# GpSimd subtracts one of the twelve weight splits of each expert

## The reference, cut to what matters

```python
def expert_block(args):
    xblk, e = args
    gu = xblk @ w_gu[e] + b_gu[e]                     # (rows, 1024) @ (1024, 2048)
    x_glu = jnp.minimum(gu[:, :F], SWIGLU_LIMIT)
    x_lin = jnp.clip(gu[:, F:], -SWIGLU_LIMIT, SWIGLU_LIMIT)
    act = x_glu * jax.nn.sigmoid(SWIGLU_ALPHA * x_glu) * (x_lin + 1.0)
    return act @ w_down[e] + b_down[e]                # (rows, 1024) @ (1024, 1024)

y = yb.reshape(P, D) * row_gate[:, None]
out = jax.ops.segment_sum(y, row_tok, num_segments=N + 1)[:N]
```

## Time and profile before

| | us |
|---|---|
| median of 3 runs | 1246.93 (1246.45 to 1248.09) |
| the profiled execution | 1246.31 |
| its span, first to last instruction | 1244.5 |
| VectorE busy | 1148.0 |
| TensorE busy (matmuls) | 1147.7 |
| ScalarE busy | 933.5 |
| GpSimd busy | 517.7 |

### The profile page before, as it was taken

The page is one execution under the profiler, slowest core; times in us unless marked ns, Lnnn a source line. Parts: engine busy times, 40 slices in busy tenths (PEclk is TensorE's granted clock), DMA queues, the critical chain, the costliest instruction groups (busy, mean ns, idle before and its releaser), DMA issues.

```text
span 1244.5 us, 40003 instructions
## 1 busy us (share of the span) xinstructions
PE 1147.7 (92%) x17556; PEld 886.6 (71%) x17557; DVE 1148.0 (92%) x870; ACT 933.5 (75%) x823; POOL 517.7 (42%) x69
## 2 busy tenths in 40 slices
PE   5999999999999999999999999999999999999974
PEld 2445545877777777777777777777777778888741
DVE  5755576999999999999999999999999999999987
ACT  5334444788888888888888888888888888888851
POOL 0110400027777776767766666632300111366620
PEclk9999999999999999999999999999999999999998
DMA  9605853899999999999999999999999999999975
GB/s 349 226 3 203 301 206 136 331 364 400 418 417 415 418 417 415 420 415 418 414 415 419 418 417 416 415 418 413 418 409 420 412 413 417 416 417 418 416 312 239
DMA packets 73255, 458.08 MB, mean 368 GB/s; under 512 B 10076, under 2 KB 10588, under 8 KB 23632
## 3 DMA queue, kind: packets, MB, share of 16 engines
q1 hardware_dynamic: 68480, 445.30, 88.3%
q0 software_dynamic: 3472, 8.21, 1.7%
q10 hardware_dynamic: 1152, 2.19, 0.5%
HBM read 443.26 MB, written 24.77 MB: 376 GB/s over the span
## 4 chain that ended last, share of the span: by engine, by line
PE 40%; DVE 34%; issue 21%; DMA 3%; ACT 2%; DVEq 0%; SPq 0%; ACTq 0%; POOLq 0%
DVE ring L415 23%; PE ps L436 15%; PE ps L472 10%; PE ps L1127 8%; PE ps L429 3%; DVE arena L502 1%; DVE arena L505 1%; PE ps L1230 1%; DVE arena L517 1%; DVE arena L508 1%; DVE arena L511 1%; ACT ring L412 1%; DMA arena<-in_x_dram 1%; DMA arena<-in_w_gu_dram 1%; PE ps L1167 1%
## 5 line engine op out<-in xcount | busy, mean ns | idle before, releaser
L494 POOL DMA_INDIRECT planes<-arena,slot_row x31 | 494.7, 15958 | 554.9 <-ACT arena L524 554.9
L415 DVE SCALAR_TENSOR_TENSOR ring<-ring 128x2048 f16<-128x2048 f32 x290 | 652.5, 2286 | 3.9 <-ACT ring L412 3.2
L412 ACT ACTIVATE ring<-ring 128x2048 f16<-128x2048 f32 x290 | 543.2, 1904 | 40.7 <-DMA ring<-in_w_gu_dram 20.9
L436 PE MATMUL ps<-arena,ring 128*128 128x88 f16 x12288 | 506.3, 205 | 43.1 <-issue 23.7
L436 PEld LDWEIGHTS ps<-arena,ring 128*128 128x128 f16 x12288 | 489.4, 100 | 53.7 <-issue 38.8
L472 PE MATMUL ps<-ring,arena 128*88 128x512 f16 x1536 | 337.5, 379 | 4.0 <-DVE arena L517 2.6
L472 PEld LDWEIGHTS ps<-ring,arena 128*88 128x88 f16 x1536 | 181.6, 120 | 146.3 <-issue 4.0
L415 DVE SCALAR_TENSOR_TENSOR ring<-arena,ring 128x2048 f16<-128x2048 f32 x94 | 212.5, 2287 | 1.1 <-ACT ring L412 0.9
L412 ACT ACTIVATE ring<-arena 128x2048 f16<-128x2048 f32 x94 | 178.5, 1904 | 13.6 <-DMA arena<-in_w_gu_dram 6.8
L429 PE MATMUL ps<-arena 128*128 128x88 f16 x2048 | 92.3, 205 | 9.1 <-issue 8.3
L429 PEld LDWEIGHTS ps<-arena 128*128 128x128 f16 x2048 | 84.5, 100 | 11.1 <-issue 11.0
(11 more groups left out here) (161 smaller groups left out, 613.5 us busy)
## 6 DMA issues: line engine op xcount, KB each, us to landing
ring<-in_w_gu_dram SPq DMA_DIRECT2D x194, 1024.0 KB, 11.6
ring<-in_w_down_dram SPq DMA_DIRECT2D x96, 1024.0 KB, 12.0
arena<-in_w_gu_dram SPq DMA_DIRECT2D x62, 1024.0 KB, 11.5
arena<-in_w_down_dram SPq DMA_DIRECT2D x32, 1024.0 KB, 13.0
ring<-in_w_in_dram SPq DMA_DIRECT2D x4, 2048.0 KB, 12.2
ring<-planes SPq DMA_DIRECT2D x6, 1024.0 KB, 11.1
ring<-in_w_out_dram SPq DMA_DIRECT2D x2, 2048.0 KB, 8.5
arena<-in_x_dram SPq DMA_DIRECT2D x4, 512.0 KB, 11.7
```

The costliest lines, as they stand in the source:

```text
L412: return act.activation(split_of(slot)[:, 0, :], raw(r), ACT.Copy, scale=SCALE_W)
L415: return dve.scalar_tensor_tensor(split_of(slot)[:, 1, :], raw(r), SCALE_W, split_of(slot)[:, 0, :], ALU.mult, ALU.subtract)
L436: mm = pe.matmul(o, w[:, i, cols], src[:, j, k, :], start=start and n == 0, stop=stop and n == 2, skip_group_check=True)
L494: return pool.indirect_dma_start(out=planes, out_offset=bass.IndirectOffsetOnAxis(ap=rows, axis=0), in_=y_row[0:SCAT, :], in_offset=None, ...
```

## The change

In stages 3 to 31 the low half of chunk 7 is no longer made by VectorE:

- ScalarE scales the raw chunk 7 by 32 in place, waits for that (`scaled`), and then copies it to the high half. That is one more 128x2048 instruction in each stage.
- GpSimd subtracts the high half from the scaled chunk (`low7`). Its program has `low7(e + 3)` right behind the scatter of expert e.
- VectorE goes from low half 6 to low half 8. Both that and GpSimd's subtraction count up `handed`; VectorE waits until both are done, and only then counts `low_ready` up by two, for chunks 7 and 8 together. Then it goes on with low half 9.

Stages 0 to 2 stay as they were.

```diff
+            def low7(s):
+                h, q = s // 2, s % 2
+                pool.wait_ge(high_ready, nth(s, 7) + 1)
+                pair_of = split_of(phase(7))
+                pool.tensor_tensor(pair_of[:, 1, :], raw(raw_slot(h, q, 7)), pair_of[:, 0, :], ALU.subtract)\
+                    .then_inc(handed, 1)
+
             def add_rows(e):
...
             for e in range(E - 1):
                 add_rows(e)
+                if e + 3 < E:
+                    low7(e + 3)
...
                 high(h, q, 4)
                 act_high_part(s - 1)
-                for c in range(5, 8):
-                    high(h, q, c)
+                high(h, q, 5)
+                high(h, q, 6)
+                if first:
+                    high(h, q, 7)
+                else:
+                    r = raw_slot(h, q, 7)
+                    act.wait_ge(slot_loaded[r], loaded(h, q, 7))
+                    act.activation(raw(r), raw(r), ACT.Copy, scale=SCALE_W).then_inc(scaled, 1)
+                    act.wait_ge(scaled, s - 2)
+                    act.wait_ge(chunk_used, nth(s, 7) - RAW + 1)
+                    act.activation(split_of(phase(7))[:, 0, :], raw(r), ACT.Copy).then_inc(high_ready, 1)
                 high(h, q, 8)
                 high(h, q, 9)
...
-            def stage(h, q, last=False):
+            def stage(h, q, last=False, by_pool=True):
...
                 act_low_part(s - 1)
-                for c in range(6, 10):
-                    low(h, q, c)
+                low(h, q, 6)
+                if by_pool:
+                    dve.wait_ge(high_ready, nth(s, 8) + 1)
+                    dve_low(dve, phase(8), raw_slot(h, q, 8)).then_inc(handed, 1)
+                    dve.wait_ge(handed, 2 * s - 4)
+                    dve.sem_inc(low_ready, 2)
+                else:
+                    low(h, q, 7)
+                    low(h, q, 8)
+                low(h, q, 9)
...
-            stage(1, 0)
+            stage(1, 0, by_pool=False)
             stage(1, 1)
```

More of the change, by code:

```diff
@@ L304, in build_program @@
         act32_ready = sem("act32_ready")
+        handed = sem("handed")
+        scaled = sem("scaled")
         ah_ready = sem("ah_ready")
```

## The result

The changed kernel takes 1310.73 us (median of 3 runs, 1310.57 to 1311.42) against 1246.93: 1.0517 times the time before, 95% interval 1.0503 to 1.0531, or 63.8 us more. The forecast was 1318, with 1293 to 1348.

What follows compares the result with a forecast made beforehand. VectorE was taken to set the 30.86 us stage, with transfers full too. Minus 2.20 for the split, plus 4.49 for the subtraction and 0.20 hand-over gave 33.35 us; +2.49 times 29, +72 us: 1318 us, range 1293 to 1348.

Steps and rivals of the forecast that it cites:

- What bounds the kernel before: Expert loop: VectorE and the transfers are both full; VectorE sets the 30.86 us stage.
- the transfers would hardly follow: Expert loop: at 416 GB/s a stage's 12.84 MB need almost 30.86 us, even if VectorE lost a whole split.
- Exclusion, 4.49 us of VectorE's time: Each stage near split 8: VectorE stands still for GpSimd's whole subtraction, 4.49 us, since both read SBUF.
- lower bound: Subtraction takes 3.93 us if L697's record held a wait for L1503: +1.6 a stage, 46 us, 1293 us.
- the sum: VectorE's stage: 30.86 - 2.20 + 4.49 + 0.20 = 33.35 us, +2.49 a stage.
- Hand-over, 0.20: VectorE's pause at `handed` each stage: 0.09 lost overlap of splits plus a good 0.1 for wake-up, 0.20 us.
- ACT's extra copy at nothing: ScalarE's 29 added scalings of chunk 7, 1.91 us each, still fit in the stage and cost nothing.
- The first ring: Rival: loop over PE, ACT and POOL between chunk 7 releases exceeds VectorE's sum; 34.3 us a stage, 1345 us; chance 0.16.
- Neither rival: The two ring rivals: over PE, ACT and POOL, 1345 us, chance 0.16; through the scatter, 1667 us, chance 0.03.
- The scatter: GpSimd's scatter, issued some 16 us later behind the subtraction, still gets in at L502 (`dve_glu`) and costs nothing.
- The ring through it: Rival: the scatter misses L502 and its 28.8 us delay the next rows; 45.4 us a stage, 1667 us; chance 0.03.
- The rows named for the test: Expected records: subtraction 4.4 to 4.6 us, stage 33.3, DMA 380 to 390 GB/s, VectorE losing 130 us in all.

Runs made afterwards that it cites:

- e1: Kernel before, but in stages 3 to 31 nobody makes chunk 7's low half, chunks 7 and 8 released together: 1247.54 us, ratio 1.0009.
- e7: Kernel before, all twelve splits on VectorE, but in stages 3 to 31 chunks 7 and 8 released together after both splits: 1254.31 us.
- e10: Changed kernel's ScalarE (scaling in place, then copy), but VectorE makes all twelve low halves in old order and GpSimd only scatters: 1246.41 us.
- e9: Changed kernel without ScalarE's scaling in place; high half 7 made in one scaled copy, GpSimd subtracts it from the unscaled chunk: 1306.53 us.

## Why the prediction was right

**What bounds the kernel before** was read rightly, and e1 shows "the transfers would hardly follow": the time stays within 0.2% with a whole split gone.

**Exclusion, 4.49 us of VectorE's time.** Right in kind, somewhat too large. Put together from the runs the stage is 30.86 - 2.20 (split 7) + 4.10 (GpSimd undisturbed) + 0.12 = 32.88, where the 0.12 is the hand-over's 0.33 less some 0.2 by which GpSimd's record overlaps the splits at its two ends. The mis-sized term is the 4.49: L697's record holds a wait of 0.4 us for L1503. It ends 3.93 us behind the end of L1503 at 36.20, and in the loop the subtraction of 611.87 ends 3.95 us behind that of split 6. The prediction had this as its lower bound and took the upper reading. 0.39 us times 29 is 11 us, more than the whole miss of 7. That the miss is no larger is luck: late stages that the sum had at nothing (below) add some 4 us on the other side, and the last stage grew by 3.9 us, not 2.5. The Trainium skill, "GPSIMD Engine Reference", section "Performance versus the Vector engine", gives 4497 ns for a float32 add of this length. For the subtraction here, with one float16 input and a float16 output, the undisturbed records say 4.10 us, and the measurement decides.

**Hand-over, 0.20.** 0.33 by itself (e7), about 0.12 net of the overlap in the changed kernel, so the sum had 0.08 too much.

**ACT's extra copy at nothing.** So it is in the order of the kernel before (e10, 1246.41 us). In the changed kernel it is not quite: e9 leaves out just this copy and gets 4.2 us back.

**The first ring** was given as hidden by 1.3 us, with 1345 us for the case that it isn't. In 28 stages it added 33.04 - 32.88 = 0.16 us on average, some 4 us in all; e9, without the scaling, is 4.2 us faster. What it does is seen at TensorE. Busy us per engine in short stretches of the kernel after, the granted clock third from the right:

```profile
617.00:619.00 2.00, 0.00 (x0) 0.00 (x0) 2.00 (x1) 2.00 (x2) 1.84 (x2) 0.71 0.98 406
619.00:621.00 2.00, 1.60 (x23) 1.61 (x24) 1.76 (x2) 2.00 (x2) 1.07 (x1) 0.50 0.48 86
621.00:623.00 2.00, 2.00 (x31) 2.00 (x29) 2.00 (x2) 0.43 (x1) 0.00 (x0) 0.50 0.74 299
```

and TensorE's timeline for chunk 7 in this stage and the next:

```profile
619.40 3.70 PE L438 MATMUL ps<-arena,ring 128*128 128x88 f16 x48 [2.87 <-DVEq L1780]
...
653.46 2.06 PE L438 MATMUL ps<-arena,ring 128*128 128x88 f16 x48 [1.48 <-DVEq L1780]
```

TensorE idles 2.87 us for the two chunks that come out together, the clock falls from 2.4 to 1.2 GHz, and chunk 7 takes 3.70 us. Behind an idle time of 1.48 it stays high and takes 2.06. The slow chunk delays the rows, those the highs, and the next stage is the one of 34.06. The other late stages agree: each of the eleven above 33 us follows a chunk 7 of 2.74 us or more, and none follows one of 2.06 or less. Neither rival's sum had this. What makes the clock fall is not settled by the length of the idle time alone, for nearly the same one was followed by the full clock:

```profile
1148.62 2.06 PE L438 MATMUL ps<-arena,ring 128*128 128x88 f16 x48 [2.83 <-DVEq L1780]
```

**The scatter** was costed rightly at nothing, for a wrong reason. It was to wait for `taken`; instead it is through at 620.07 (issued at 617.29, record 2.78 us, landing about 10 us behind its issue), since VectorE now pauses at the hand-over, at 619.28. ScalarE, which waited for it before (1.36 us in the earlier trace rows), has no such wait from 400 to 1100 us. The ring through it is out.

**The rows named for the test** came in the main: stage 33.0 (33.3), 391 GB/s (380 to 390), and the stalls. The subtraction's rows did not: 4.10 us, or 5.19 to 5.58 with their wait, for 4.4 to 4.6. Split time over 2.29 us each is (632.2 + 255.5) - 355 x 2.29 = 75 us, idle time before splits 45, 120 in all for 130.

## What to carry to other kernels

Before work goes to an idle engine, ask whether the two may run at the same time, and look for a place in the trace where they already overlap: one stretched record is worth more than a share of 42% busy. GpSimd work that reads SBUF belongs beside VectorE instructions that take an input from PSUM (L1498 and `taken` kept their lengths) or in VectorE's pauses; behind back-to-back instructions with two inputs in SBUF it waits, and then VectorE does. No run here had a VectorE instruction with a single input, in SBUF, beside it. And ask first what is full besides the engine to be relieved: here the transfers were, so that even a free subtraction would have brought nothing.

## What was not expected of the hardware

- A GpSimd fill (128x2048, 1.80 us) runs beside a two-input VectorE instruction at full speed, while a copy (1.89 us) and a subtraction (4.10 us) stop it. Before the runs the rows only told of the subtraction.
- An idle time of 2.87 us on TensorE came with half the clock from 618.0 to 624.5 us; one of 1.48 us did not, and neither did one of 2.83 us at another place. These runs don't show what decides it.
- The chain of work that ended last ran 71% over PE and ACT, and yet only 4 of the 64 us were got back by shortening that ring: 32.92 us of the stage were VectorE's own.
